# Token-grouped expert gathers, 128x32 stationary operands and straight-line code in a hybrid trunk

## What is computed

```python
def block(xb):                      # 128 tokens
    q = (xb @ w_q).reshape(PEER_BLOCK, PEER_HEADS, 2, PEER_QDIM // 2)
    s = jnp.einsum('thpd,hpnd->thpn', q, sub_keys).astype(f32)
    s1, i1 = lax.top_k(s[:, :, 0], PEER_TOPK)
    s2, i2 = lax.top_k(s[:, :, 1], PEER_TOPK)
    ...
    top_s, pos = lax.top_k(cand, PEER_TOPK)
    e_idx = jnp.take_along_axis(cand_idx, pos, axis=-1)
    gate = jax.nn.softmax(top_s, axis=-1)
    u_sel = u[e_idx]
    v_sel = v[e_idx]
    act = jax.nn.gelu(jnp.einsum('thkd,td->thk', u_sel, xb).astype(f32), approximate=False)
    return jnp.einsum('thk,thkd->td', (gate * act).astype(xb.dtype), v_sel)
```

## Time and profile before

| | us |
|---|---|
| median of 3 runs | 5041.36 (5039.62 to 5042.62) |
| span of the profiled execution | 5039.4 |
| PE busy | 4091.1 (81%) |
| DVE busy | 2610.4 (52%) |
| POOL busy | 2089.5 (41%) |
| ACT busy | 1595.9 (32%) |
| gathers of `uv` | 1024, 1073.81 MB |

### The profile page before, as it was taken

The page is one execution under the profiler, slowest core; times in us unless marked ns, Lnnn a source line. Parts: engine busy times, 40 slices in busy tenths (PEclk is TensorE's granted clock), DMA queues, the critical chain, the costliest instruction groups (busy, mean ns, idle before and its releaser), DMA issues.

```text
span 5039.4 us, 51891 instructions
## 1 busy us (share of the span) xinstructions
PE 4091.1 (81%) x12452; PEld 1979.0 (39%) x12452; DVE 2610.4 (52%) x5380; ACT 1595.9 (32%) x4254; POOL 2089.5 (41%) x2276
## 2 busy tenths in 40 slices
PE   5699999997877777777776999999877777777777
PEld 2387444453323233222234864454532322323222
DVE  5843235146656656654467422351566566566444
ACT  2121222123443443433322222130234434434333
POOL 4622000005656655666555210000066556556664
PEclk8899999998989899899987999999999899888999
DMA  6300111128999999999952001111299999999997
GB/s 221 111 1 1 43 63 63 59 85 332 410 364 393 387 370 393 388 398 409 394 194 84 1 1 55 63 51 59 100 376 404 365 396 385 373 391 393 403 411 316
DMA packets 223721, 1222.88 MB, mean 243 GB/s; under 512 B 18240, under 2 KB 59840, under 8 KB 89024
## 3 DMA queue, kind: packets, MB, share of 16 engines
q0 software_dynamic: 147456, 1073.81, 53.1%
q1 hardware_dynamic: 76096, 147.10, 8.3%
HBM read 1218.74 MB, written 2.10 MB: 242 GB/s over the span
## 4 chain that ended last, share of the span: by engine, by line
issue 28%; PE 21%; POOL 15%; DVE 14%; DMA 8%; PEld 5%; DVEq 3%; ACT 3%; PEldq 2%; POOLq 2%; ACTq 0%; SPq 0%
POOL reg L1777 8%; DMA reg<-uv,e_ic 7%; POOL e_ic L1774 7%; PE bank L888 4%; PE bank L456 3%; PEld bank L456 3%; PE bank L567 2%; DVE reg L1590 2%; DVE reg L1677 2%; PE bank L558 2%; PEld bank L749 1%; DVE reg L1585 1%; PE bank L649 1%; PE bank L821 1%; PE bank L630 1%
## 5 line engine op out<-in xcount | busy, mean ns | idle before, releaser
L888 PE MATMUL bank<-reg,hT 128*128 128x512 f32 x4096 | 2032.0, 641 | 625.7 <-ACT hT L1195 621.5
L1677 DVE CUSTOM_DVE_ANT_0 reg<-reg 128x1024 f32<-128x1024 f32 x1024 | 1256.6, 1227 | 1062.8 <-DMA reg<-uv,e_ic 940.8
L1777 POOL DMA_INDIRECT reg<-uv,e_ic x1024 | 1206.9, 1179 | 850.0 <-POOL e_ic L1774 754.0
L888 PEld LDWEIGHTS bank<-reg,hT 128*128 128x128 f32 x4096 | 783.2, 202 | 1873.4 <-ACT hT L1195 1074.0
L1774 POOL COPY e_ic<-e_idx 128x1 uint32 x1024 | 481.6, 470 | 1521.8 <-DVEq L1655 1292.3
L1189 ACT ACTIVATE reg<-reg 128x1 f32<-128x1 f32 x1024 | 207.2, 202 | 1397.3 <-DVEq L1678 1395.6
L456 PE MATMUL bank<-hT,reg 128*128 128x512 f32 x1120 | 497.5, 598 | 10.6 <-issue 8.4
L1195 ACT ACTIVATE hT<-con,reg 128x128 f32<-128x128 f32 x1024 | 411.2, 402 | 70.8
L456 PEld LDWEIGHTS bank<-hT,reg 128*128 128x128 f32 x1120 | 211.8, 191 | 286.3 <-issue 286.1
L1191 ACT ACTIVATE reg<-reg 128x1 f32<-128x1 f32 x1024 | 301.5, 294 | 70.4
L1755 POOL TENSOR_TENSOR reg<-reg,con 128x512 f32<-128x512 f32 x112 | 141.0, 1272 | 378.8 <-ACTq L1014 218.7
(11 more groups left out here) (260 smaller groups left out, 3851.0 us busy)
## 6 DMA issues: line engine op xcount, KB each, us to landing
reg<-w_ada SPq DMA_DIRECT2D x36, 1024.0 KB, 5.2
reg<-w_mac SPq DMA_DIRECT2D x16, 1536.0 KB, 6.8
reg<-w_in SPq DMA_DIRECT2D x10, 2048.0 KB, 7.7
reg<-uv,e_ic POOLq DMA_INDIRECT x1024
reg<-w_ada SPq DMA_DIRECT2D x6, 2048.0 KB, 11.6
reg<-w_mb SPq DMA_DIRECT2D x8, 1536.0 KB, 6.9
reg<-w_out SPq DMA_DIRECT2D x4, 2048.0 KB, 8.2
reg<-w_pq SPq DMA_DIRECT2D x4, 2048.0 KB, 7.8
```

Of the source, the lines that this page charges most:

```text
L888: last = mm(acc[j][:, :], e_diag[:, s_, :], e_row[s_][:, D + j * NB:D + (j + 1) * NB], start=False, stop=False)
L1677: V.tensor_tensor_reduce(e_row[s_][:, 0:D], e_row[s_][:, 0:D], e_hc, 1.0, 0.0, ALU.mult, ALU.add, e_dot[:, s_:s_ + 1])
L1777: pool.indirect_dma_start(e_row[s_], None, uv, bass.IndirectOffsetOnAxis(ap=e_ic[:, s_:s_ + 1], axis=0))\
```

## The change

Four things change together.

1. All loops of the five instruction streams are written out, those over the layers, the tiles and the groups. Wait values are then constants.
2. A gather no longer brings one slot of 128 tokens, but 4 slots of 32 tokens: partitions 32s to 32s+31 hold slot s of the same 32 tokens. The number of gathers (128 for a tile), their size (128 rows of 8 KB) and the number of row buffers (8) stay. To this end DVE writes expert numbers and gates in a new layout, by 16 copies of 32 partitions each (`i4`, `g4`), and ACT writes four copies of 32 tokens to `e_hc`, once for each group of 32 tokens (`spread`). POOL reads its indices straight from `e_idx`; the copy to `e_ic` and the wait for it are gone.
3. Gathers are handled in batches of four (`PER`), 32 batches to a tile. `rows_used`, `dots` and `weights` count batches: POOL may issue the four gathers of a batch when PE is through with the batch before the last, ACT makes its four weights when all four dot products are there, and PE starts when all four weight matrices are.
4. The stationary operand of the product with v is 128x32 (`sel`, four identity matrices of 32 above each other, scaled by the weights), and the four gathers of a batch go to the four 32-column strips of the PE array, each with its own 32 partitions of the two PSUM banks. After eight batches the sums of 32 tokens are complete: ACT copies them (`copied_sum`), and PE adds the four strips and transposes them in one go, by eight products with `sel` (`moved`).

The diff, cut to its core:

```diff
 GRP = 8
-NGRP = EH * ET // GRP
-PIECES = (1, 3, 4, 6, 8, 9, 11, 13)
+TOK, PER = 32, 4
+NG, NBAT = P // TOK, SLOTS // PER // 4
+BAT = NG * NBAT
+PIECES = (2, 5, 8, 11, 15, 18, 22, 26)
...
-            with sp.Fori(0, depth) as l:
+            for l in range(0, depth):
...
                 def expert_tile(lap, more, t=None):
...
-                    def groups(g0, g1):
-                        with pe.Fori(g0, g1) as g:
-                            for s_ in range(GRP):
-
-                                pe.wait_ge(diags[s_], lap * NGRP + g + 1)
-                                for j in range(2):
-                                    last = mm(acc[j][:, :], e_diag[:, s_, :], e_row[s_][:, D + j * NB:D + (j + 1) * NB], start=False, stop=False)
-                                last.then_inc(rows_used[s_], 1)
...
+                    def batch(b):
+                        turn = lap * BAT + b
+                        first, last_b = b % NBAT == 0, b % NBAT == NBAT - 1
+                        if first and turn:
+                            pe.wait_ge(acc_copied, turn // NBAT)
+                        pe.wait_ge(weights, turn + 1)
+                        for half in range(2):
+                            for q in range(PER):
+                                i = turn % 2 * PER + q
+                                last = mm(acc[half][q * TOK:(q + 1) * TOK, :], e_w[:, i, :],
+                                          e_row[i][:, D + half * NB:D + (half + 1) * NB], start=first, stop=last_b)
+                        last.then_inc(rows_used, 1)
+
+                    def moved(j):
+
+                        pe.wait_ge(acc_copied, lap * NG + j + 1)
+                        for half in range(2):
...
+                                last = mm(ps[:, i * P + j * TOK:i * P + (j + 1) * TOK], e_acc[:, k * P:(k + 1) * P], sel[:], start=True, stop=True)
...
+                        pe.drain().then_inc(acc_moved, 1)
...
+                def spread(lap, t, j):
+
+                    for s_ in range(PER):
+                        A(e_hc[j % 2][s_ * TOK:(s_ + 1) * TOK, :], e_h[j * TOK:(j + 1) * TOK, t, :], ACT.Copy)
+                    act.drain().then_inc(h_spread, 1)
...
-                            A(e_gc, e_gate[:, bass.ds(t * SLOTS + g * GRP, GRP)], ACT.Copy)
-                            for s_ in range(GRP):
-                                act.wait_ge(dots[s_], turn + 1)
-                                A(e_ge[:, s_:s_ + 1], e_dot[:, s_:s_ + 1], ACT.Gelu)
-                                act.drain()
-                                A(e_wg[:, s_:s_ + 1], e_gc[:, s_:s_ + 1], ACT.Copy, scale=e_ge[:, s_:s_ + 1])
-                                act.drain()
-
-                                act.wait_ge(rows_used[s_], turn + 1)
-                                A(e_diag[:, s_, :], ident, ACT.Copy, scale=e_wg[:, s_:s_ + 1]).then_inc(diags[s_], 1)
...
+                    def batch(b):
+                        turn = lap * BAT + b
+                        j, g0 = b // NBAT, b % NBAT * PER
+                        o = turn % 2 * PER
+                        act.wait_ge(dots, turn + 1)
+                        A(e_ge[:, o:o + PER], e_dot[:, o:o + PER], ACT.Gelu)
+                        act.drain()
+                        for q in range(PER):
+                            A(e_wg[:, o + q:o + q + 1], g4[:, t, j, g0 + q:g0 + q + 1], ACT.Copy, scale=e_ge[:, o + q:o + q + 1])
+                        act.drain()
+
+                        if turn >= 2:
+                            act.wait_ge(rows_used, turn - 1)
+                        for q in range(PER):
+                            A(e_w[:, o + q, :], sel[:], ACT.Copy, scale=e_wg[:, o + q:o + q + 1])
+                        act.drain().then_inc(weights, 1)
...
+                        for j in range(NG):
+                            for s_ in range(PER):
+                                V.tensor_copy(i4[s_ * TOK:(s_ + 1) * TOK, t, j, h0 * PER:h1 * PER],
+                                              e_n1[j * TOK:(j + 1) * TOK, h0 * ET + s_:h1 * ET:PER])
...
-                                dve.wait_ge(rows_landed[s_], 16 * (turn + 1))
-
-                                dve.wait_ge(rows_used[s_], turn + 1)
-                                V.tensor_tensor_reduce(e_row[s_][:, 0:D], e_row[s_][:, 0:D], e_hc, 1.0, 0.0, ALU.mult, ALU.add, e_dot[:, s_:s_ + 1])
-                                dve.drain().then_inc(dots[s_], 1)
...
+                        for q in range(PER):
+                            i = turn % 2 * PER + q
+                            dve.wait_ge(rows_landed[i], 16 * (turn // 2 + 1))
+                            V.tensor_tensor_reduce(e_row[i][:, 0:D], e_row[i][:, 0:D], e_hc[b // NBAT % 2], 1.0, 0.0, ALU.mult, ALU.add, e_dot[:, i:i + 1])
+                        dve.drain().then_inc(dots, 1)
...
-                                pool.wait_ge(rows_used[s_], turn + 1)
-                                pool.tensor_copy(e_ic[:, s_:s_ + 1], e_idx[:, bass.ds(t * SLOTS + g * GRP + s_, 1)]).then_inc(idx_ready, 1)
-                                pool.wait_ge(idx_ready, turn * GRP + s_ + 1)
...
+                        if turn >= 2:
+
+                            pool.wait_ge(rows_used, turn - 1)
...
+                            g = t * SLOTS + b * PER + q
+                            pool.indirect_dma_start(e_row[i], None, uv, bass.IndirectOffsetOnAxis(ap=e_idx[:, g:g + 1], axis=0))\
+                                .then_inc(rows_landed[i], 16)
```

More of the change, by code:

```diff
@@ L460, in _ @@
             pe.wait_ge(loaded, 64)
-            with pe.Fori(0, depth) as l:
+            for l in range(0, depth):
                 def adaln(part):
@@ L904, in _ @@
-                with pe.Fori(0, TT - 1) as t:
+                    def batch(b):
[10 more added lines that the diff above has]
+                        last.then_inc(rows_used, 1)
@@ L905, in _ @@
+                    acc = [psum[T.bank(("acc", half))] for half in range(2)]
+                    for b in range(BAT):
+                        batch(b)
+                        if more and b == 0:
+                            for q in range(2):
+                                score(lap + 1, T, l * (TT - 1) + t, q)
+                        if b % NBAT == NBAT - 1:
+                            moved(b // NBAT)
+                for t in range(0, TT - 1):
                     expert_tile(l * TT + t, True, t)
@@ L940, in _ @@
             act.drain()
-            with act.Fori(0, depth) as l:
+            for l in range(0, depth):
                 act.nop().then_inc(G["cond_ready"].sem, 1)
@@ L1196, in expert_tile @@
-                    groups(0, 1)
-                    if more:
-                        A(e_qc, e_q[:, :, bass.ds((t + 1) * P, P)], ACT.Copy)
-                        act.drain().then_inc(E_["tile_in"].sem, 2)
-                        for q in range(2):
-                            scores(T, l * (TT - 1) + t, q)
-                        groups(1, PIECES[5] + 1)
-                        soft(lap + 1)
-                        groups(PIECES[5] + 1, NGRP)
-                    else:
-                        groups(1, NGRP)
@@ L1207, in expert_tile @@
-                    for j in range(2):
-                        ps = full(("acc", j), lap, T)
-                        A(e_acc[:, j * NB:(j + 1) * NB], ps[:, :], ACT.Copy).then_inc(T.freed(("acc", j)), 1)
-                    act.drain().then_inc(E_["acc_copied"].sem, 1)
-                with act.Fori(0, TT - 1) as t:
+                    def batch(b):
[13 more added lines that the diff above has]
+                        act.drain().then_inc(weights, 1)
@@ new lines, in copied_sum @@
+                    def copied_sum(j):
+                        turn = lap * BAT + (j + 1) * NBAT
+                        act.wait_ge(rows_used, turn)
+                        if lap or j:
+                            act.wait_ge(acc_moved, lap * NG + j)
+                        for half in range(2):
+                            A(e_acc[:, half * NB:(half + 1) * NB], psum[T.bank(("acc", half))][:, :], ACT.Copy)
+                        act.drain().then_inc(acc_copied, 1)
+                    for b in range(BAT):
+                        batch(b)
+                        j = b // NBAT
+                        if more and b == 0:
+                            A(e_qc, e_q[:, :, (t + 1) * P:(t + 2) * P], ACT.Copy)
+                            act.drain().then_inc(E_["tile_in"].sem, 2)
+                            for q in range(2):
+                                scores(T, l * (TT - 1) + t, q)
+                        if b % NBAT == 2:
+                            if j < NG - 1:
+                                spread(lap, t, j + 1)
+                            elif more:
+                                spread(lap + 1, t + 1, 0)
+                        if more and b == PIECES[5]:
+                            soft(lap + 1)
+                        if b % NBAT == NBAT - 1:
+                            copied_sum(j)
@@ L1241, in _ @@
```

(14 more changed lines are left out.)

113 lines of the change are left out of this document (46 added, 67 removed).

## The result

The changed kernel takes 5359.7 us (median of 4, 5351.2 to 5364.7) against 5040.5 beside it on the same chip (4 runs): ratio 1.0628, 95% interval 1.0610 to 1.0645. The forecast was 5178 us in a range of 4985 to 5300. The direction was right and so was the kind of cause, but the loss is 310 us in the profiled executions (5349.4 against 5039.4) where the four terms of the sum made 135, and the time lies above the range.

A forecast was written before the change was run, and what follows sets the result against it. DMA bandwidth was taken as nearly the bound before, the release path as the bound after. The terms summed as 5039.4 + 2.0 + 160 - 40 + 33 - 18 = 5176, stated as 5178 us, range 4985 to 5300.

The forecast's parts named there:

- a batch takes the greater of 9.96 and R / 2: Expert stages: a batch lasts the longer of four transfers (9.96 us) and half the buffer round; forecast 10.9 us.
- R: Expert stages: the loop from one issue to the next issue into the same buffers, summed to 21.8 us.
- issue to first dot product: First part of a batch's round, from POOL's issue to DVE's start, taken from a stall: 5.96 us.
- term 1: Plain batches in the expert stages: tiles of 348 against 326.1 us, +20 for each of 8, +160 us.
- Term 2: Routing pieces and tile ends: 16 against 25 us a tile, six such tiles, with a margin for copies, -40 us.
- Term 3: Start and end of each expert stage: later first dot product, more copies, DMA silence, later drain; two layers, +33 us.
- Term 4: Straight-line code: the second layer's restart, 6.71 us on DVE, and register arithmetic go; -18 us, bounds 0 and -40.
- The 0.81 us for PE to issue: Last part of a batch's round, from PE to POOL's next issue, read off what stands before it in the old kernel.
- The three gaps of 2.6 us: A batch's round: the three dot products after its first follow at 2.6 us each, 7.8 in all; range 2.49 to 3.0.
- ACT's upper bound: ACT's part of a batch's round, every operation at its own length without overlap: 3.35 us; 2.25 was taken.
- the fast rival: Expert stages: the DMA queue stays full, so the kernel gets faster, about 4990 us; chance 0.22.
- Serial strips: PE's products: strips not four abreast, about 5610 us two at a time, 6450 one after another; chance 0.08.

The follow-up runs named there:

- per gather: The changed kernel with handshakes for each gather instead of each batch of four: 4972.2 us, ratio 0.9865.
- release by four: The changed kernel with dot products starting as each gather lands, but the next four issued only once all four earlier gathers are used: 5130.6 us.
- half of the products: The changed kernel with products of v columns 512 to 1023 left out in seven of each eight batches: 5223.9 us, ratio 1.0360.
- strip by strip: The changed kernel with the two loops around its matmuls exchanged, both halves of a slot before the next slot: 5370.7 us, ratio 1.0651.

## Why the prediction was right or wrong

**Right: what bounds the kernel, and what takes over.** The bound was the DMA queue, the release path took its place, PEclk fell to 0.55, strips ran abreast, gathers came in fours. Plain tiles fell to 0.94 and 365 GB/s, where 0.92 and 375 were foreseen. The loss vanishes with the batching and with nothing else that was tried.

**Wrong: "a batch takes the greater of 9.96 and R / 2", with 5.96 for issue to first dot product.** This is the step that failed, in term 1: issue to first dot product measured 7.36, not 5.96, and R 23.04, not 21.8. The 5.96 came from a gather that had nothing left to wait for in the queue: its first packet started 2.16 us after its issue, 0.36 after the last landing before it. In the loop a batch is issued 3.6 us before the other's last dot product, its packets stand behind the other's, and both ends of the gap cost extra. By the packet records of the plain tiles, the landings of a batch follow each other by 3.29, 2.48, 2.49 and 3.24 us, 11.5 in all, where a full queue gives 2.51 four times. Of the 1.46 us too much, 0.65 is idle time of the 16 DMA engines and 0.8 is slower packets: those of the first gather of a batch fill 2.97 us of each engine, those of the second 2.73, against 2.51. It is so in every kernel where the queue ran empty: first gather behind a gap of over 0.3 us 2.96 to 3.10 us per engine in each kernel's mean (12 gaps in before, 49 in after), and the last gather ahead of the gap lands 2.9 to 3.7 us after the one before it, not 2.5, with engines idle that a full queue would have filled. Why packets behind a gap are slower is not settled by these runs. So near the crossing the step lies above both bounds:

| kernel | by the terms, R / 2 | greater of it and 9.95 | measured, inner plain batches |
|---|---|---|---|
| per gather | - | 9.95 | 10.05 |
| release by four | about 9.5 | 9.95 | 10.4 |
| half of the products | 10.1 | 10.1 | 10.94 |
| after | 10.9 | 10.9 | 11.5 |

**Term 1, plain batches: +160, measured +353** (a plain tile grew by 42.2 and 46.0, eight times their mean). 0.6 us a batch is what the step above missed, 154 us in 256 batches. Of the other 39, about 15 are the 2 us a tile that I had taken off for the old tiles, and most of the rest is the tile's boundary, where four batches take about 48 us, not four inner steps of 11.5 less the 1 us that I gave the prefetch.

**Term 2, pieces and tile ends: -40, measured -62**, what the six tiles with pieces grew less than plain ones (27.6, 27.3, 33.8, 34.1, and the two first tiles 42.6 and 37.3, against 44.1). Its reason, that a loop that already waits hides part of a piece, is not shown: the four tiles that had stood behind a jump back make 54 of the 62, and there the written-out code alone gives 37; the first tiles grew nearly as much as plain ones.

**Term 3, start and end: +33, measured +19.** The first dot product of layer 0 stands at 1157.4 against 1145.93, +11.5, that of layer 1 +7.1, the end +0.6: I had counted the first batch's delayed release here, and it lies in the first tile.

**Term 4, written-out code: -18, measured 0 in the mixer**, so the step from DVE's 6.71 us to the time was wrong: the first gather of layer 1 came no sooner without the pause. Alone, the written-out code is worth -46, but at the starts of tiles, where term 2 had it. The sum closes: 353 - 62 + 19 + 0 = 310.

**Luck, and sums that were wrong.** The 0.81 us for PE to issue was read off POOL's wait for its own copy, not for PE; that PE's release takes 0.84 is luck. The three gaps of 2.6 us came out as 7.69 in all, but by their landings as 2.5, 2.5 and 3.2. The range was too narrow by its own terms: ACT's upper bound alone gives 0.55 x 256 = 141 us more and the landing's alone 0.6 x 256 = 154, so either alone passes the 5300 of the range, by 19 and 32 us, and below the forecast ACT's bound gives 0.2, not 0.55. In the sum of the fast rival the pieces stand at -25, in the words before it at -50. The best window of rows 7 is 427 GB/s, not 422.

**The rivals.** The changed kernel did not have the full queue; its forms with handshakes for each gather and each pair did. The way there that I named (PE at 2.4 GHz, its term 1.98, R = 20.1) is too weak: with that term at 2.10 the kernel with half of the products still takes 5223.9 us, not 4990. Serial strips are out by the 3.64 us. For that, the rule on the strips in the Trainium skill (TensorE: Matmul & The Clock Gate, Measured speedup vs the span model), 2.38 times for three, would have made a burst 4.6 us; 3.64 measured is 3.7 times faster than 16 x 0.85 us of single instructions, and rows of four start 0.85 us apart, the full factor of four, in float32.

**POOL's issue.** The other page, the Trainium skill (SBUF — State Buffer, Who interferes with whom), lets a DVE instruction with two SBUF inputs block a GpSimd one that reads SBUF, and infers that descriptor generation is spared. Here an issue that begins inside a dot product ends 0.81 us after that dot product, in the middle eight tenths of the 380 cases that begin more than 0.1 us before its end 0.81 to 0.82, and takes 0.94 otherwise; in the round above 2490.31 + 1.96 = 2492.27 and the dot product that ran ended at 2491.47. The issue is held off like the copy was; that it would be spared is wrong. It befalls all four issues of a batch about alike, but only the first of each four stands in R.

## What to carry to other kernels

A ring of buffers that feeds a saturated DMA queue should be released in the smallest unit that the consumers allow: with eight buffers, singles kept the queue nearly full through a tile with pieces (DMA share 0.99), pairs only where nothing disturbed it, and fours never did. Treat a round as safe only when it is well under what the ring takes to transfer; within a tenth of that, the steps here were 0.5 to 0.8 us a batch above both bounds. And look for the issuing engine's own round: where it equals a transfer's length, it can't catch up after a stall, and taking a copy of 0.2 us (0.7 beside a dot product) and its wait out of it was worth 83 us.

## What the runs showed of the hardware

- Matmuls to four column strips overlap whatever their order in the program: 16 in 3.64 us with strips in turn, 3.67 us strip by strip, at 1.2 GHz; 1.93 us at 2.4 GHz. A later instruction to a free strip starts ahead of an earlier one to a busy strip: inferred from start times 13 to 17 ns apart, then 0.85 us, since the records do not name strips. The Trainium skill (TensorE: Matmul & The Clock Gate, The mechanism) says that matmuls start strictly in program order; the trace of the strip by strip kernel disagrees, if its instructions stand in the order in which they are written.
- Emptying the gather queue costs more than its idle time: packets of 8 KB of the first gather behind a gap take 0.37 to 0.39 us in the mean, 0.31 in a full queue. Why is open.
- A pause of 6.3 to 7.1 us on DVE where a loop jumps back cost 8 us a time (10.4 - 2.2), since POOL stood behind it and the queue behind POOL; the same pause in the mixer cost nothing.
